# Norm boundaries of a two-block transformer kernel handled in two pairs of row blocks

## What is computed

```
def rms_norm(x, g):
    return x * rsqrt(mean(x * x, axis=-1) + 1e-6) * g

def first_block(x):
    z = rms_norm(x, g_pre_mix) @ w_in                       # norm1
    merged = gates(z) * mixers(z)                           # three branches
    x = x + rms_norm(merged @ w_o, g_post_mix)              # post1
    hf = rms_norm(x, g_pre_ffn)                             # norm2
    gate, up = split(hf @ w_ffn_in)
    return x + rms_norm((silu(gate) * up) @ w_ffn_out, g_post_ffn)   # post2

def layer(x, l):                                            # l = 0, 1
    shift, scale, gate = split(silu(c) @ w_ada[l] + b_ada[l])
    h = rms_norm(x, norm_w[l]) * (1 + scale) + shift        # layer norm
    merged = attention_and_retention(h @ w_in[l])
    return x + gate * (merged @ w_out[l])

out = rms_norm(layer(layer(first_block(x), 0), 1), final_norm_w)
```

## Time and profile before

| | us |
|---|---|
| median of 3 runs | 2788.69 |
| the profiled execution: its time | 2789.3 |
| its span | 2787.6 |
| TensorE busy | 2653.7 |
| VectorE busy | 1208.9 |
| ScalarE busy | 967.1 |
| GpSimd busy | 405.7 |

### The profile page before, as it was taken

The page is one execution under the profiler, slowest core; times in us unless marked ns, Lnnn a source line. Parts: engine busy times, 40 slices in busy tenths (PEclk is TensorE's granted clock), DMA queues, the critical chain, the costliest instruction groups (busy, mean ns, idle before and its releaser), DMA issues.

```text
span 2787.6 us, 33179 instructions
## 1 busy us (share of the span) xinstructions
PE 2653.7 (95%) x12845; PEld 2207.5 (79%) x12861; DVE 1208.9 (43%) x1592; ACT 967.1 (35%) x1254; POOL 405.7 (15%) x433
## 2 busy tenths in 40 slices
PE   7999999999998999997999999999989999999997
PEld 6887778777886778786788888888778888888885
DVE  5435554645524665634333333443343333343434
ACT  6435444236233322213433333223243333323223
POOL 3103333100000100000301001331030000032300
PEclk9989999999999999999999999999999999999998
DMA  5210003222242454522222223222213222322221
GB/s 211 75 61 18 14 16 117 91 80 76 97 175 76 162 184 149 183 76 91 91 98 99 90 96 106 87 83 89 91 62 106 90 90 96 124 93 81 89 101 51
DMA packets 43494, 269.31 MB, mean 97 GB/s; under 512 B 5304, under 2 KB 5424, under 8 KB 16000
## 3 DMA queue, kind: packets, MB, share of 16 engines
q1 hardware_dynamic: 31536, 226.51, 23.6%
q0 software_dynamic: 11280, 39.31, 4.0%
q10 hardware_dynamic: 576, 2.10, 0.2%
HBM read 265.80 MB, written 2.10 MB: 96 GB/s over the span
## 4 chain that ended last, share of the span: by engine, by line
PE 70%; issue 19%; DVE 5%; POOL 4%; ACT 2%; DMA 0%; DVEq 0%; POOLq 0%; ACTq 0%
PE PS L1781 67%; POOL merged L577 1%; PE PS L1970 1%; DVE w_split L1094 1%; ACT w_split L614 1%; POOL res_hi L571 1%; POOL res_lo L571 1%; POOL merged L516 1%; DVE small L1339 0%; PE PS L1860 0%; DVE R L1427 0%; DVE h_act L1102 0%; DVE xres L1151 0%; ACT R L627 0%; ACT R L637 0%
## 5 line engine op out<-in xcount | busy, mean ns | idle before, releaser
L1781 PE MATMUL PS<-h_act,w_split 128*128 128x512 f32 x5472 | 1266.3, 393 | 13.6 <-DVEq L1106 7.2
L1781 PEld LDWEIGHTS PS<-h_act,w_split 128*128 128x128 f32 x5472 | 1034.2, 189 | 230.7 <-DVE h_act L1102 6.9
L1094 DVE TENSOR_TENSOR w_split<-raw,w_split 128x2048 fp32r<-128x2048 f32 x215 | 508.1, 2363 | 963.4 <-ACT w_split L614 947.4
L614 ACT ACTIVATE w_split<-raw 128x2048 fp32r<-128x2048 f32 x215 | 411.6, 1914 | 868.2 <-PE PS L1781 861.2
L1781 PE MATMUL PS<-w_split,h_act 128*128 128x512 f32 (+1 forms) x1728 | 416.3, 391 | 24.0 <-DVE h_act L1102 19.9
L1781 PEld LDWEIGHTS PS<-w_split,h_act 128*128 128x128 f32 x1728 | 317.9, 192 | 82.7 <-DVE h_act L1102 14.0
L1781 PE MATMUL PS<-y_act,w_split 128*128 128x512 f32 x1152 | 265.3, 391 | 2.2 <-DVE w_split L1094 2.2
L1781 PEld LDWEIGHTS PS<-y_act,w_split 128*128 128x128 f32 x1152 | 217.3, 189 | 47.9 <-DVE w_split L1094 2.6
L1781 PE MATMUL PS<-R 128*128 128x128 f32 (+3 forms) x896 | 190.5, 364 | 9.7 <-ACT R L997 5.5
L1781 PEld LDWEIGHTS PS<-R 128*128 128x128 f32 x896 | 135.3, 201 | 42.7 <-issue 15.5
L1781 PE MATMUL PS<-w_split,res_hi 128*128 128x384 f32 x512 | 130.6, 336 | 0.0
(11 more groups left out here) (273 smaller groups left out, 2130.9 us busy)
## 6 DMA issues: line engine op xcount, KB each, us to landing
raw<-in_weights SPq DMA_DIRECT2D x214, 1024.0 KB, 4.9
R<-in_w_ada POOLq DMA_DIRECT2D x36, 512.0 KB, 4.8
gate_bc<-in_w_ada POOLq DMA_DIRECT2D x12, 512.0 KB, 4.7
xres<-in_x ACTq DMA_DIRECT2D x4, 512.0 KB, 5.9
R<-in_nsa_wk POOLq DMA_DIRECT2D x1, 2048.0 KB, 9.7
xres<-in_x POOLq DMA_DIRECT2D x1, 2048.0 KB, 10.8
R<-in_decay POOLq DMA_DIRECT2D x8, 256.0 KB, 3.3
out<-R SPq DMA_DIRECT2D x4, 512.0 KB, 3.0
```

Source lines behind the costliest of these rows:

```text
L614: act.activation(w_split[:, 0, half, :, :], raw[:, half, :, :], ACT.Copy).then_inc(w_hi, 1)
L1094: dve.tensor_tensor(w_split[:, 1, half, :, :], raw[:, half, :, :], w_split[:, 0, half, :, :].bitcast(F32), ALU.subtract).then_inc(w_lo, 1)
L1781: return pe.matmul(out, lhsT, rhs, start=start, stop=stop, skip_group_check=True)
```

## The change

Norm1, norm2 and the two layer norms go by two pairs of row blocks. The row-major groups swap sets, so that a last group writes banks 0 to 3 and the transposes have banks 4 to 7, one pair of row blocks at a time (256 tokens, two k-tiles in a bank). The first pair's 16 transposes stand inside the last group, 8 matmuls before its end (`last_group`). The next block's first group (`first_group`) is done in two token halves of 256 columns, 96 matmuls each; the second pair's 16 transposes stand inside the first half, behind 28 of its 32 steps. High and low parts are made in pieces of 256 columns, in two passes; the orders of ScalarE and VectorE are rewritten around them. `modulated` moves from R0 to M1 and holds one token half. A dummy square root loads the Sqrt table ahead of a boundary. The final norm has no transposes, no scaled rows and no split behind it: VectorE applies reciprocal root and gain in one operation per block, and the last block is written in two halves. The layer loop on ScalarE, VectorE and TensorE and the FFN loops on TensorE are written out. The last dummy load of weights goes. The diff, cut to its core:

```diff
-            for tb in range(TB):
+            for tb in range(TB - 1):
                 sp.wait_ge(out_ready, tb + 1)
                 sp.dma_start(a["out"][0, tb * P:(tb + 1) * P, :], row0[:, tb, :]).then_inc(out_done, 16)
-            sp.wait_ge(out_done, 16 * TB)
+            for n in range(2):
+                sp.wait_ge(out_ready, TB + n)
+                sp.dma_start(a["out"][0, (TB - 1) * P:, n * W:(n + 1) * W], row0[:, TB - 1, n * W:(n + 1) * W]
+                             ).then_inc(out_done, 16)
+            sp.wait_ge(out_done, 16 * (TB + 1))
...
-            def norm_hi(rows, gain):
-
-                for kt in range(KT):
-                    act.wait_ge(rows_done, 2 * rows + kt + 1)
-                    act.activation(h_act[:, 0, kt, :], PS[:, kt, :], ACT.Copy, scale=vecs[:, gain + kt:gain + kt + 1]
-                                   ).then_inc(hi_made, 1)
+            def norm_hi(name, rows, gain, part, kts):
+                for kt in kts:
+                    if kt < 4:
+                        act.wait_ge(rows_done, 2 * rows + 4 * part + kt + 1)
+                    else:
+                        act.wait_ge(act_lo, at(name).l + KT * part + kt - 3)
+                    act.activation(h_act[:, 0, kt, 256 * part:256 * part + 256],
+                                   PS[:, 4 + kt % 4, kt // 4 * 256:kt // 4 * 256 + 256], ACT.Copy,
+                                   scale=vecs[:, gain + kt:gain + kt + 1]).then_inc(hi_made, 1)
+            def modulate(l, part, kts):
+                if part:
+                    act.wait_ge(act_lo, at("layer.norm", l).l + KT)
+                for kt in kts:
+                    act.wait_ge(rows_done, 2 * (ROWS["layer"] + TB * l) + 4 * part + kt % 4 + 1)
+                    act.activation(modulated[:, kt, :], PS[:, 4 + kt % 4, kt // 4 * 256:kt // 4 * 256 + 256], ACT.Identity,
+                                   bias=mod_cols[:, 0, kt:kt + 1], scale=mod_cols[:, 0, KT + kt:KT + kt + 1]
+                                   ).then_inc(full_ready, 1)
+            def root_table():
+                act.activation(spare, cf[:, C_ONE:C_ONE + 1], ACT.Sqrt)
...
-            def post_norm(posts, k, rows, second_half, ahead):
-
+            def post_norm(posts, k, rows, second_half, g, hi):
+                root_table()
                 second_half(0)
                 second_half(1)
                 post_root(posts, 0)
@@ -669,18 +689,22 @@
                 root(k, 0)
                 root(k, 1)
                 scaled(rows, 0)
-                ahead()
                 scaled(rows, 1)
+                split_hi(g, 0)
                 second_half(2)
                 post_root(posts, 2)
+                hi(0, range(4))
                 second_half(3)
                 post_root(posts, 3)
+                split_hi(g, 1)
                 post_square(posts, 2)
+                hi(0, range(4, KT))
                 root(k, 2)
+                scaled(rows, 2)
                 post_square(posts, 3)
-                scaled(rows, 2)
                 root(k, 3)
                 scaled(rows, 3)
+                hi(1, range(KT))
...
+            act.wait_ge(vecs_ps, 1)
+            act.activation(vecs[:, :], PS[:, 0, 0:V_END], ACT.Copy).then_inc(vecs_ready, 1)
+            release(0, vecs_ready, 1)
+            split_hi(0, 0)
+            act.wait_ge(vecs_ready, 1)
+            norm_hi("norm1", ROWS["norm1"], V_G1, 0, range(KT))
+            split_hi(0, 1)
             arrived(2)
             arrived(3)
             root(VARS["norm1"], 2)
             root(VARS["norm1"], 3)
             scaled(ROWS["norm1"], 2)
             scaled(ROWS["norm1"], 3)
-            act.wait_ge(vecs_ps, 1)
-            act.activation(vecs[:, :], PS[:, 0, 0:V_END], ACT.Copy).then_inc(vecs_ready, 1)
-            release(0, vecs_ready, 1)
-            split_hi(0, 0)
-            act.wait_ge(vecs_ready, 1)
-            norm_hi(ROWS["norm1"], V_G1)
-            split_hi(0, 1)
+            norm_hi("norm1", ROWS["norm1"], V_G1, 1, range(KT))
...
+                root_table()
+                if l == LAYERS - 1:
+                    for tb in range(TB):
+                        second_half(tb)
+                        root(k, tb)
+                    break
...
+            def norm_lo(c, gain, part, kts):
+                for kt in kts:
+                    cols = slice(256 * part, 256 * part + 256)
+                    dve.wait_ge(hi_made, c.h + KT * part + kt + 1)
+                    dve.scalar_tensor_tensor(h_act[:, 1, kt, cols], PS[:, 4 + kt % 4, kt // 4 * 256:kt // 4 * 256 + 256],
+                                             vecs[:, gain + kt:gain + kt + 1], h_act[:, 0, kt, cols].bitcast(F32),
+                                             ALU.mult, ALU.subtract).then_inc(act_lo, 1)
+                if part:
+                    release(1, act_lo, c.l + 2 * KT)
+            def modulated_split(own, l, part, kts):
+                cols = slice(256 * part, 256 * part + 256)
+                before = None
+                for kt in list(kts) + [None]:
+                    if kt is not None:
+                        dve.wait_ge(full_ready, 2 * KT * l + KT * part + kt + 1)
+                        own.put(dve.tensor_copy(h_act[:, 0, kt, cols], modulated[:, kt, :]))
+                    if before is not None:
+                        dve.wait_ge(own_layer, own.n - (kt is not None))
+                        low(h_act[:, 1, before, cols], modulated[:, before, :], h_act[:, 0, before, cols])
+                    before = kt
...
-            def post_norm(own, posts, k, rows, second_half, second_gained, ahead):
+            def post_norm(own, posts, k, rows, second_half, second_gained, g, lo):
                 second_half(0)
                 second_half(1)
@@ -1165,19 +1207,23 @@
                 variance(rows, 1)
                 inverse(k, rows, 0)
                 inverse(k, rows, 1)
-                ahead()
+                split_lo(g, 0)
                 second_half(2)
                 post_variance(posts, 2)
                 second_gained(2)
-                post_add(own, posts, 2)
+                lo(0, range(4))
                 second_half(3)
                 post_variance(posts, 3)
                 second_gained(3)
+                post_add(own, posts, 2)
+                split_lo(g, 1)
                 variance(rows, 2)
                 post_add(own, posts, 3)
                 inverse(k, rows, 2)
+                lo(0, range(4, KT))
                 variance(rows, 3)
                 inverse(k, rows, 3)
+                lo(1, range(KT))
...
+                own.link(dve.tensor_tensor(row0[:, tb, W:], PS[:, tb, :], second_gain, ALU.mult))
+                if tb == TB - 1:
+                    dve.sem_inc(set_free[0], 1)
...
+                if l < LAYERS - 1:
+                    modulation(l + 1)
                 split_lo(c.g + 1, 0)
                 def update(n, tb, done):
                     half = slice(n * W, (n + 1) * W)
                     dve.wait_ge(bank_done, 4 * (c.g + n) + tb + 1)
-                    own.link(dve.tensor_tensor(stage[:, tb, :], PS[:, 4 * n + tb, :], gate_bc[:, half], ALU.mult))
+                    own.link(dve.tensor_tensor(stage[:, tb, :], PS[:, 4 * (1 - n) + tb, :], gate_bc[:, half], ALU.mult))
+                    if tb == TB - 1:
+                        dve.sem_inc(set_free[1 - n], 1)
                     dve.tensor_tensor(xres[:, tb, half], xres[:, tb, half], stage[:, tb, :], ALU.add).then_inc(done, 1)
...
+                if l == LAYERS - 1:
+                    dve.wait_ge(gain_in, 16 * (GAINS["final"] + 1))
+                    for tb in range(TB):
+                        update(1, tb, x_ready)
+                        mean(tb)
+                        inverse(k, rows, tb)
+                        dve.wait_ge(rstd_ready, rows + tb + 1)
+                        for lo, width in [(0, DM)] if tb < TB - 1 else [(0, W), (W, W)]:
+                            dve.scalar_tensor_tensor(row0[:, tb, lo:lo + width], xres[:, tb, lo:lo + width],
+                                                     rstd[:, tb:tb + 1], gains[:, GAIN_SLOT["final"], lo:lo + width],
+                                                     ALU.mult, ALU.mult).then_inc(out_ready, 1)
+                    break
...
                 split_lo(c.g + 2, 0)
                 update(1, 2, x_ready)
+                modulated_split(layer_own, l + 1, 0, range(4))
+                update(1, 3, x_ready)
                 mean(2)
+                split_lo(c.g + 2, 1)
                 inverse(k, rows, 2)
-                update(1, 3, x_ready)
-                dve.sem_inc(set_free[1], 1)
                 mean(3)
+                modulated_split(layer_own, l + 1, 0, range(4, KT))
                 inverse(k, rows, 3)
-                own.end()
-            dve.wait_ge(gain_in, 16 * (GAINS["final"] + 1))
-            for tb in range(TB):
-                dve.wait_ge(xn_ready, ROWS["final"] + tb + 1)
```

(56 more changed lines are left out.)

133 lines of the change are left out of this document (48 added, 85 removed).

## The result

| | before | after |
|---|---|---|
| median of the runs | 2788.61 us (4 runs, 2787.76 to 2791.43) | 2765.92 us (4 runs, 2764.38 to 2766.28) |
| span of the profiled run | 2787.6 us | 2764.6 us |

The ratio is 0.9916, 95% interval 0.9899 to 0.9933. The forecast was 2768.4 us (2760 to 2778): the change gained 22.7 us where I had reckoned 20.3. Run once more beside the later experiments, the changed kernel came to 2765.49 us (2762.92 to 2766.37).

A forecast was written before the change was run, and what follows sets the result against it. TensorE was taken to bound the kernel, busy 2653.7 of 2787.6 us, so its stops and slow stretches were to be had. 8.3 + 6.2 + 3.9 + 3.9 - 2.0 = 20.3 us off 2788.7 gave 2768.4 us (2760 to 2778).

The forecast's parts named there:

- 256 columns at 0.12 us: Price of one 256-column matmul in the token halves: 23.0 for 21.7 us, +1.3 us for each of four groups.
- the rival that counted 0.19 a load: Weight loads of 256-column matmuls don't overlap: a group takes 36.5 us, the kernel 2822 us; chance 0.06.
- the upper price from 280 columns: Upper bound for 256-column matmuls, from the row of 280 columns: +3.1 us for a group, 2775.6 us in all.
- norm2, 8.3: Feed-forward's norm: TensorE idles 3.9 us for banks 0 to 3, group ends at 930.4, before 939.1; gain 8.3 us.
- First layer norm, 6.2: TensorE waits 3.2 us inside the last group, then idles 6.7; the next ends at 1347.9 against 1354.1, gain 6.2 us.
- the waits for low parts 4 and 7: First layer norm: low part 4 comes only at 1327.9, hiding about 2 us of lower clock; 1330.1 after low part 7.
- Second layer norm, 3.9: Group ends at 2077.9 against 2081.8, gain 3.9 us, which includes ScalarE's 2.66 us stop at the loop's turn.
- Tail, 3.9: End of kernel: no last split or scaling, root and gain in one pass, half the last transfer; gain 3.9 us.
- Start, loss of 2.0: Start: group 1's weight split comes later, behind low parts and small tables, at 52.7; loss 2.0 us (0 to 3).
- the signs of being wrong: 256-column matmuls above 0.13 us, clock of 0.5 behind transposes after dense work, or stops without releaser in written-out loops.
- Clock by transposes: Rival: transposes inside dense work let the clock fall, about 1 us lost behind each of seven sets: 2775 us; chance 0.10.
- Release later than reckoned: Rival: VectorE and ScalarE release later, 3 to 4 us more on each of three boundaries: 2779 us; chance 0.14.

The follow-up runs named there:

- e3: The changed kernel with banks 0 to 3 given back before VectorE makes the first pair's low parts, at norm2 and both layer norms: 2763.78 us.
- e4: The kernel before with only its loops written out (layer loop on ScalarE, VectorE and TensorE; TensorE's feed-forward loops): 2784.73 us, ratio 0.9985.
- e7: The changed kernel with the old tail (ScalarE scales the rows, VectorE's gain apart, last row block in one transfer): 2769.2 us.
- e1: The changed kernel with norm1 done as before the change (all four row blocks transposed, then a group of 512-column matmuls): 2759.72 us.
- e9: The changed kernel with 58 unused transposes of the identity put ahead of group 1 at the start, where TensorE idles 6.95 us: 2763.41 us.
- e8: The changed kernel without the early dummy square root that ScalarE makes ahead of each boundary: 2773.24 us.
- e8b: The changed kernel without the early dummy square root, run again beside the changed kernel: 2772.63 us, against 2765.49 us.

## Why the prediction was right

- **What bounds, and 256 columns at 0.12 us.** Right: 108 of them with what they wait for take 13.19 us, 0.122 each. A load for each of them costs no more than that, so the rival that counted 0.19 a load is dead, and the upper price from 280 columns with it. The loads are busy all the time (27.48 of 27.50 us), so they may well be what sets the 0.122; no run parts loads from matmuls.
- **norm2, 8.3.** Measured 8.2. No wait for the transposes, as said; then the release of banks 0 to 3, 2.9 us of idling where I had 3.9. The first 84 matmuls then took 11.8 us where I had 10.4, with the clock at 0.50 from 911 to 914 us: I had charged 0.4 for it, and the two errors cancel. e3 shows that low parts stand right beside the release.
- **First layer norm, 6.2.** Measured 7.7. The wait inside the group (3.2 forecast) was 2.8, the idle stretch 5.75 (forecast 6.7, though its own times, 1313.1 and 1319.6, give 6.5). Then the waits for low parts 4 and 7, which were to hide the lower clock, did not show: 84 matmuls of 256 columns ran in 12.97 us without a stop that the trace shows. The term was too small by the release that came earlier and by these waits.
- **Second layer norm, 3.9.** Measured 4.8. Here the mechanism was weighed wrongly: e4 gets 4.3 us from writing out the loops alone, 2.0 of them by the clock, so the pairs bring some 0.5 on top. I had booked ScalarE's stop as part of the gain and not asked what the old order would do without it.
- **Tail, 3.9.** Measured 5.0; e7 splits it in 2.9 and 2.1. VectorE was through about when I had it (5.7 us after TensorE's last matmul, forecast 6.0). The mis-sized part is the way out of the last half block: 2.4 us from VectorE's end to the end of the span, where I had 3.3 and the whole block took 3.6.
- **Start, loss of 2.0.** The mis-sized term. The order of VectorE's work was right (tables to 49.4, split to 51.7, forecast 52.7), but the clock was left out: TensorE idles 6.95 us there and the clock goes to 0.50. Group 1 starts 1.7 us later than before (51.81 against 50.1), what follows the three groups 4.6; by e1 the start costs 6.2. I charged a low clock after the idle stretches at the norms and not after the longest one. That error (2.6) and the understated gains (1.5 + 0.9 + 1.1), with the feed-forward's chance gain of 1.9, cancelled to 2.8 us of the span. (0.8 us more lost between the start and norm2 and 0.9 gained in layer 0, neither forecast, cancel too.) So the closeness of the total is partly luck; the mechanism at norm2 and the first layer norm, the waits and where they stand, is not.
- **The signs.** The first group of norm2 starts 6.7 us after the first pair's transposes begin (forecast about 6), group 1 at the start waits for VectorE's split, and the tail from the last matmul is 8.1 us (forecast 9, before 13). Of the signs of being wrong none was seen.
- **Clock by transposes.** The rival did not come true: in 921 to 923, 1327 to 1329 and 2049 to 2051 us transposes inside dense work ran 16 in 1.91 us, and the next matmuls took 0.122. The Trainium skill ("TensorE: Matmul & The Clock Gate", Part 4: PE-mode transpose) says that transposes don't engage the full clock; in e9 58 transposes with nothing else, behind dense matmuls, kept 1.00, so here the trace disagrees.
- **Release later than reckoned.** It was earlier at the first two norms (2.9 and 5.75 us of idling for 3.9 and 6.7) and as reckoned at the second layer norm (3.0 for 3.1).

## What to carry to other kernels

When work is moved forward, look at whose cover it leaves: group 0 began 5.7 us earlier than with the old order (e1) and group 1, bound by VectorE, 5.4 us later, and behind the new idle stretch the clock fell. Price each new idle stretch of TensorE with its clock. Measure an edit of a few us over several runs and follow the landmarks of two traces, since low-clock stretches worth 1.65 us each came and went here in places that the edit didn't touch. When a change bundles several edits, try the smallest alone: writing out the loops was worth 4 us by itself, the place inside the last group nothing measurable, and leaving the start as it was would have saved 6 more.

## What the runs showed of the hardware

- The same wait of 2.2 us of TensorE was followed by a clock of 1.00 or of 0.50: 1.00 when TensorE went on at 1004.10 (after) and 1004.50 us (e7), 0.50 at 1004.32 (e8) and 1004.55 (e8b). What decides it, these runs don't tell. Such falls, inside the layers, go with 3.8 of the 7 us that a table load of 1.28 us, made early, was worth.
- ScalarE stood still for 2.66 us at a hardware loop's turn; written out, 0.63 us, for TensorE's transposes.
- 58 transposes of a 128x128 identity (6.49 us, 0.11 us each), right behind dense matmuls, held the granted clock at 1.00.
- Up to the last matmul the clock's lack adds up to 53 to 72 us of a span of 2757 to 2788 in the seven traces of the table, in kernels in which TensorE is busy for 95 to 96%.
